# Opening stage: the modulation weights as the moving side of the matmul, in four groups of 32 output partitions

## The reference, cut to what matters

```python
sc, sc_ctx = silu(c), silu(c_ctx)                     # two vectors of 1024
mx = split((sc @ w_mod[i] + b_mod[i]), 6)             # six vectors of 1024 for the latents
mc = split(sc_ctx @ w_mod[i] + b_mod[i], 6)           # and for the context
h = modulate(rms_norm(x, gain), mx[0], mx[1])         # modulate(t, shift, scale) = t * (1 + scale) + shift
```

## Time and profile before

| | us |
|---|---|
| median of three runs | 5378.92 |
| lowest and highest run | 5378.86, 5384.19 |
| the profiled execution | 5388.18 |
| its span, first to last instruction | 5386.5 |

### The profile page before, as it was taken

How to read it: one execution, slowest core, us unless ns; L and a number is a source line. 1 busy time by engine, 2 the same in 40 slices (tenths; PEclk the granted TensorE clock), 3 DMA queues, 4 the chain that set the end, 5 groups by cost and what they waited for, 6 DMA issues and landing times. The chain is left out here.

```text
span 5386.5 us, 86380 instructions
## 1 busy us (share of the span) xinstructions
PE 4443.9 (83%) x35544; PEld 3748.2 (70%) x35544; DVE 2462.8 (46%) x3440; ACT 1467.3 (27%) x2453; POOL 589.1 (11%) x797
## 2 busy tenths in 40 slices
PE   7667799999976588859988686499999976657998
PEld 6434488888843488839977465388888874435997
DVE  3444443335455544444444323343337836664444
ACT  2144431223243221122213312221123323332222
POOL 2011100001112322210001000000001103320000
PEclk7788899999997799969998755699999986668999
DMA  3255422222376622033323222222222334342332
GB/s 130 92 177 168 149 63 63 60 65 82 104 239 216 216 45 51 23 104 94 94 64 102 84 67 72 100 63 63 59 61 81 108 99 139 128 148 78 94 90 75
DMA packets 688777, 540.01 MB, mean 100 GB/s; under 512 B 129501, under 2 KB 613986, under 8 KB 688449
## 3 DMA queue, kind: packets, MB, share of 16 engines
q1 hardware_dynamic: 659200, 444.63, 27.6%
q0 software_dynamic: 29248, 90.63, 4.7%
HBM read 451.04 MB, written 84.11 MB: 99 GB/s over the span
## 5 line engine op out<-in xcount | busy, mean ns | idle before, releaser
L86 PE MATMUL acc<-h_hi,w_hi 128*128 128x258 f32 (+2 forms) x4416 | 1402.2, 318 | 46.2 <-DVE h_lo L455 39.6
L88 PE MATMUL acc<-h_hi,w_lo 128*128 128x258 f32 (+2 forms) x4416 | 1398.4, 317 | 0.0
L87 PE MATMUL acc<-h_lo,w_hi 128*128 128x258 f32 (+2 forms) x4416 | 1396.8, 316 | 0.0
L86 PEld LDWEIGHTS acc<-h_hi,w_hi 128*128 128x128 f32 x4416 | 832.7, 189 | 113.9 <-DVE h_lo L455 23.5
L87 PEld LDWEIGHTS acc<-h_lo,w_hi 128*128 128x128 f32 x4416 | 833.5, 189 | 60.5 <-issue 0.5
L88 PEld LDWEIGHTS acc<-h_hi,w_lo 128*128 128x128 f32 x4416 | 833.0, 189 | 59.0
L334 ACT CAST w_hi<-staged 128x1024 fp32r<-128x1024 f32 (+1 forms) x414 | 407.6, 1030 | 574.6 <-PE acc L88 391.1
L442 DVE TENSOR_TENSOR w_lo<-staged,w_hi 128x1024 fp32r<-128x1024 f32 (+1 forms) x414 | 480.5, 1200 | 137.7 <-ACT w_hi L334 135.1
L86 PE MATMUL acc<-hidden_hi,w_hi 128*128 128x512 f32 (+1 forms) x1200 | 419.9, 350 | 66.3 <-DVE hidden_lo L573 66.3
L483 DVE COPY offset<-acc 128x2 f32<-128x2 f32 x276 | 43.8, 159 | 927.2 <-PE acc L88 924.5
L87 PE MATMUL acc<-hidden_lo,w_hi 128*128 128x512 f32 (+1 forms) x1200 | 419.5, 350 | 0.0
(11 more groups left out here) (449 smaller groups left out, 6846.2 us busy)
## 6 DMA issues: line engine op xcount, KB each, us to landing
staged<-in_w_ffn_in SPq DMA_DIRECT2D x88, 512.0 KB, 4.5
staged<-in_ffn_w_in SPq DMA_DIRECT2D x88, 512.0 KB, 4.6
wmod<-in_w_mod SPq DMA_DIRECT2D x8, 3072.0 KB, 11.3
wmod<-in_mod_w SPq DMA_DIRECT2D x8, 3072.0 KB, 13.1
wmod<-in_mod_w SPq DMA_DIRECT2D x16, 1536.0 KB, 9.6
rows<-acum SPq DMA_DIRECT2D x48, 512.0 KB, 3.9
staged<-in_ssd_w_in SPq DMA_DIRECT2D x42, 512.0 KB, 4.5
wmod<-in_w_mod SPq DMA_DIRECT2D x8, 2048.0 KB, 8.1
```

Source lines behind the costliest of these rows:

```text
L86: nc.tensor.matmul(out, w[0], x[0], start=start, stop=False)
L87: nc.tensor.matmul(out, w[0], x[1], start=False, stop=False)
L88: return nc.tensor.matmul(out, w[1], x[0], start=False, stop=stop)
```

## The change

In `opening` the two sides of the modulation product change places. The condition tile with its 32 columns is stationary and 128 columns of weights move, one matmul for each of the four column tiles of a quarter, each into partitions 32j to 32j + 31 of `sums[:, s, :]`; the loop over the 8 slices is now the outer one. The result is rows: partition 32j + b holds the sums of condition b for column tile 4s + j. When all four quarters are done, VectorE copies the whole of `sums` (128 x 512) to `mod_rows`, TensorE turns it with four 128x128 transposes into the PSUM buffer `turned[0]` (named `columns`), and VectorE's two additions take partition-wise columns 32j + b from there. Two semaphores (`rows_kept`, `columns_ready`) and the waits for them are new, and a wait for all token copies ahead of the four transposes. `sums` grows from 128 x 32 to 128 x 512 values. `MOD_GROUPS = 4` moves to the top of the file.

```diff
-        sums = ps("sums", [P, 2 * KD, 2])
+        sums = ps("sums", [P, n_mod, P])
+        mod_rows = sb("mod_rows", [P, n_mod, P])
+        columns = turned[0]
...
                     pe.wait_ge(S[f"w_loaded{s}"], 16)
-                    for j in range(NC // P):
-                        for k in range(KD):
-                            mm = nc.tensor.matmul(sums[:, s * (NC // P) + j, :], wbuf[s][:, k, j * P:(j + 1) * P], conds[0][:, k, 0:2],
+                    for k in range(KD):
+                        for j in range(MOD_GROUPS):
+                            mm = nc.tensor.matmul(sums[32 * j:32 * j + 32, s, :], conds[0][:, k, :], wbuf[s][:, k, j * P:(j + 1) * P],
                                                   start=(k == 0), stop=(k == KD - 1))
...
+                pe.wait_ge(S["rows_kept"], 1)
+                pe.wait_ge(S["turned_used"], 2 * len(tokens))
+                for s in range(n_mod):
+                    tr = nc.tensor.transpose(columns[:, s, :], mod_rows[:, s, :], ident[:])
+                tr.then_inc(S["columns_ready"], 1)
...
                 dve.wait_ge(S["summed"], 1)
+                nc.vector.tensor_copy(mod_rows[:], sums[:]).then_inc(S["rows_kept"], 1)
                 dve.wait_ge(S["vec_used"], len(packs))
+                dve.wait_ge(S["columns_ready"], 1)
                 for b in range(2):
-                    nc.vector.tensor_tensor(modT[:, 0:2 * KD, b], sums[:, :, b], b_cols[:, 0:2 * KD], ALU.add)
+                    nc.vector.tensor_tensor(modT[:, 0:2 * KD, b].rearrange("p (s j) -> p s j", s=n_mod),
+                                            columns[:].rearrange("p s (j c) -> p s j c", c=32)[:, :, :, b],
+                                            b_cols[:, 0:2 * KD].rearrange("p (s j) -> p s j", s=n_mod), ALU.add)
```

More of the change, by code:

```diff
@@ L18 @@
 CTX = 256
+MOD_GROUPS = 4
 LAT = 512
@@ L691, in opening @@
         small = [ps(f"small{i}", [P, P]) for i in range(2)]
-        sums = ps("sums", [P, 2 * KD, 2])
+        sums = ps("sums", [P, n_mod, P])
+        mod_rows = sb("mod_rows", [P, n_mod, P])
+        columns = turned[0]
         names = ["ident_loaded", "tables_loaded"] + [f"vec_loaded{i}" for i in range(len(packs))] + [f"w_loaded{s}" for s in range(n_mod)] \
             + [f"rows_loaded{i}" for i in range(len(tokens))] + ["vec_turned", "vec_used", "turned_ready", "turned_used", "cleared",
-                                                                 "cond_ready", "summed"]
+                                                                 "cond_ready", "summed", "rows_kept", "columns_ready"]
         with stage(nc, *names) as (block, *sems):
@@ L992, in _ @@
                     pool.wait_ge(stored[s], 16 * ((tiles + 1 - s) // 2))
-MOD_GROUPS = 4
 @dataclass
```

## The result

The changed kernel takes 5336.88 us (median of 4 runs, 5329.23 to 5338.55) beside 5378.89 before (5372.10 to 5384.19): ratio 0.9919, 95% interval 0.9907 to 0.9931, 42 us less. It was measured twice more, each time beside the kernel before: 0.9925 (0.9913 to 0.9938) and 0.9921 (0.9908 to 0.9935). Forecast were 31.7 us and 5347; the time lies 3 us under the range's lower end (about 5340). The two profiled executions differ by more, 5388.18 and 5336.80.

What follows compares the result with a forecast made beforehand. TensorE's modulation product was taken to bound the opening: blocks shrink 52.1 to 15.2 us (36.9 out), less 2.0 tail, 2.25 waits and about 0.9 overlap, leaving 31.7; 5378.92 - 31.7 = 5347.2 us, range about 5340 to 5358.

Steps and rivals of the forecast that it cites:

- Block of 3.8 us at half clock: Opening's modulation product: 64 records per weight quarter take 3.8 us at the lower clock, before 10.87 to 13.81.
- Landings stay: Opening: the four weight quarters still land at 11.6, 20.4, 28.4 and 37.4 us.
- Tail 2.01: Opening's new end after the product: copy 0.69 us, TensorE's wake 0.19, four turnings 1.13.
- The lower level for all of the opening: TensorE's clock stays at 1.2 GHz throughout the opening, since TensorE idles more there after the change.
- rival 1: The clock rises in the opening, which then ends at 41.2 us: shift 34.6, whole 5344.3 us; chance 0.30.
- E: Opening's end, the start of VectorE's two last additions: 75.82 us before, forecast 44.15 after.
- Rival 2: Product's column groups don't overlap: 20.6 us a quarter, opening ends at 109.1, whole 5412 us, slower; chance 0.02.
- Rival 3: Next stage gives about 10 us back because its clock rises some 20 us later: 5357 us; chance 0.10.
- its opening is the same as any other's, as far as one trace tells, so I take the shift off both: One trace's opening stands for all runs: 31.7 us off the profiled execution (5356.5) and the median (5347.2).
- the shift: How much earlier the opening ends: 75.82 - 44.15 = 31.7 us.
- what E gains, the kernel gains, unless the next stage gives it back: The opening's end is on the path, so its 31.7 us come off the whole time.

Runs made afterwards that it cites:

- the one with 60 turnings: Changed kernel plus 60 unused 32x32 turnings on TensorE before the first weights land: 5354.45 us, beside 5347.59 for the changed kernel.
- tail alone: Kernel before, old product kept, plus only a 128x512 copy and four turnings of it, result unused: 5376.69 us, ratio 0.9986.
- 5 turnings: Kernel before plus 5 unused 32x32 turnings on TensorE before the first weights land: 5375.59 us beside 5386.35, ratio 0.9983.

## Why the prediction was right and wrong

Direction, place and mechanism were right, step by step:
- *Block of 3.8 us at half clock*: 3.64; 1.95 at full clock, as in the earlier trace rows. *Landings stay*: quarter 3 released TensorE at 37.82, forecast 37.4; the one before it came 1 us late (29.44, forecast 28.4). *Tail 2.01*: 1.98 at half clock, 1.52 at full.
- *The lower level for all of the opening*: wrong in part. The clock rose in some blocks of each trace, not in the same ones, so rival 1 held in half: in two of the openings (the first trace and the one with 60 turnings) TensorE waited for the last quarter (1.99 and 1.53 us), and E came out at 41.07 to 42.80, at rival 1's 41.2 or up to 1.6 above it, under my 44.15. That is about 2 us.
- *Rival 2* fell; the rule of the Trainium skill that a weight load overlaps only with other row groups ("TensorE: Matmul & The Clock Gate", Part 3) would have it so, and these rows contradict it: in 1.95 us stand 64 loads and 64 streams that differ only in columns, and even with neighbours in one column group a record took 0.093 us at the full clock.
- *Rival 3* fell: from the next stage's first load to the clock's rise there are 28.4 us (43.92 to 72.3), before 29.5.

The range failed, and two steps of the prediction made it fail, the second above all: the first alone would have left the time inside it. The first is "its opening is the same as any other's, as far as one trace tells, so I take the shift off both". E of the old product in six traces (without the added tail) is 75.82, 79.50, 79.01, 71.58, 77.92 and 72.82: mean 76.1, spread 8 us, by the number of blocks in which the clock rose. E after is 42.0 in the mean of three. The shift so is 34.2, not 31.7.

The second is "what E gains, the kernel gains, unless the next stage gives it back": I looked for what could return, not for what could move, and the range's lower end left 4 us for all later stages. The change also makes TensorE's list longer by about ten instructions ahead of all that follows, and the recurrence stage answers to where its code lies. Its length in 14 traces:

| TensorE's list against the kernel before | recurrence stage, us | of it weight loads idle, us |
|---|---|---|
| as before, or 256 more (3 traces) | 444.6, 445.2, 447.5 | 69.2 to 72.3 |
| some 10 more: changed kernel and its variants, tail alone, 5 turnings (9 traces) | 430.9, 436.3, 438.3, 439.2, 439.9, 440.2, 440.6, 441.0, 441.5 | 58.1 to 65.6 |
| some 130 more (2 traces) | 449.1, 452.6 | 71.6, 72.7 |

The means are 445.8, 438.6 and 450.8 us; of idle time 71.0, 63.0 and 72.2. So the stage is 7.2 us shorter, by its idle time 8.0, and that is the lucky place of the code, no merit of the change. That 130 more are worse than none is not shown: their idle time is the same, and the times of the kernel before agree (1.0001). The rest of the kernel, outside the opening and this stage, takes 4840 to 4852 us in all 14 traces, with means of 4845, 4846 and 4848 by group. 34.2 and 7.2 make 41.4, and 42.0, 42.6 and 41.9 were measured. That this agrees to 1 us is partly luck: each term is a difference of means of a few traces, which lie up to 8 us apart for E and 11 for the stage.

What is shown: the added instructions alone shorten the stage, the gaps move with the list and return after 256 instructions, and the stage of the changed kernel lengthens by 8 to 11 us beside its second and third trace when they are moved on. That TensorE stands at these gaps for a transfer of 16384 bytes of instructions is borne out by the traces, though no run changed the transfer itself. That one stands beside a gap says little, since 91 or 92 of them run in the stage, most of them beside none. But in the 14 traces there are 168 gaps of over 1 us without a releaser ahead of loads other than `one<-x,lev` (the stage's first 33 loads and the loop's branch left out), and at every one of them the loads resume 1.2 to 1.6 us after such a transfer has landed; at the loop's branch it is 1.8 to 1.9 us in all 14; ahead of `one<-x,lev`, 123 gaps, it is anything from 0.1 to 4.3. It fits the Trainium skill (Advanced Engine Details and Errata, ISA Cache: 16 KB lines, 256 instructions each). Open is why only some of these transfers come too late. Open, too, is what raises the clock in one block and not in the next.

## What to carry to other kernels

With few rows on one side of a matmul, let the narrow side be stationary and the weights stream, spread over four column groups with the loop over groups innermost: here 13.8 us became 3.6 at the lower clock, and with the loops the other way a block took 5.95 us in place of 1.95 at the full one. A change early in a long program moves all code behind it; where a stage of many short instructions follows, forecast several us for that (here the whole moved by -5 to -9 with ten more instructions, by +8 in the changed kernel with 120 more, and not at all with 128 or 256 in the kernel before), and test it with a few idle instructions before an effect is put down to the edit. One trace's opening is one draw of the clock: take the spread of runs into the step's own term.

## What was not expected of the hardware

- At the places where TensorE waits for its own instructions it resumes 1.2 to 1.6 us after 16384 bytes of them have landed, 168 times in 14 traces, and a loop's branch back costs it 3.6 to 4.5 us.
- Ten unused TensorE instructions made the kernel 0.17% faster (0.9983, 0.9974 to 0.9992); 128 made no difference (1.0001), 256 neither (1.0003).
- The clock's rise: the same block of narrow matmuls took 10.55 to 13.81 us from one execution to the next, with TensorE busy throughout.
- The granted clock's rows say 1.00 until the first recorded step, whatever the records' lengths: in the second trace of the kernel before they say so from the first block to the last (79.4 us), over four blocks at the lower clock's 13.65 to 13.81.
